# First stage of a streaming encoder step: the scale of tile t+1 ahead of tile t, second halves of the rides two products later, gate columns with hi and lo weights in one stationary

## The reference

```
n = RMSNorm(x) * g_in
z = n @ w_in                      # 2048 x (q, k, v: 3 x 1024; gate: 8; ga, u, gs: 3 x 1024)
logf = log_sigmoid(z[:, gate] + b_f)
# then attention with the cumulated logf, a state-space layer on u, output projections, norms
```

## Time and profile before

| | |
|---|---|
| median of 3 runs | 2473.47 us (2468.51, 2473.47, 2474.2) |
| profiled execution | 2475.24 us, span 2473.5 |
| PE busy | 2272.9 us, 92% of the span |
| LDWEIGHTS busy | 2138.9 us, 86% |
| DVE, ACT, POOL busy | 1593.3, 781.4, 317.3 us |
| mean granted clock of PE | 0.968 |

### The profile page before, as it was taken

How to read it: one execution, slowest core, us unless ns; L and a number is a source line. 1 busy time by engine, 2 the same in 40 slices (tenths; PEclk the granted TensorE clock), 3 DMA queues, 4 the chain that set the end, 5 groups by cost and what they waited for, 6 DMA issues and landing times. The chain is left out here.

```text
span 2473.5 us, 43304 instructions
## 1 busy us (share of the span) xinstructions
PE 2272.9 (92%) x16025; PEld 2138.9 (86%) x16025; DVE 1593.3 (64%) x2934; ACT 781.4 (32%) x1651; POOL 317.3 (13%) x350
## 2 busy tenths in 40 slices
PE   3989999999899999999688877888999999999996
PEld 3989999999899999999577757886888888999996
DVE  6768766776777878884377754755445666334664
ACT  6442333333433333333465534321001113001112
POOL 0011000000112112111233314200001110001110
PEclk9999999999999999999799888998999999999998
DMA  7474444444767788774455524435445446434332
GB/s 236 143 241 113 133 130 129 146 136 136 263 196 213 216 229 229 218 222 128 167 167 172 163 68 181 149 124 175 119 114 164 121 112 200 115 107 130 107 104 97
DMA packets 399412, 390.28 MB, mean 158 GB/s; under 512 B 73896, under 2 KB 341704, under 8 KB 392800
## 3 DMA queue, kind: packets, MB, share of 16 engines
q1 hardware_dynamic: 354176, 271.50, 38.1%
q0 software_dynamic: 20704, 77.95, 9.6%
q10 hardware_dynamic: 24384, 38.87, 4.9%
HBM read 257.56 MB, written 122.01 MB: 153 GB/s over the span
## 5 line engine op out<-in xcount | busy, mean ns | idle before, releaser
L745 PE MATMUL acc<-t_act,w_hi 128*128 128x264 f32 x5376 | 889.3, 288 | 20.0 <-DVE zb L1321 8.0
L745 PEld LDWEIGHTS acc<-t_act,w_hi 128*128 128x128 f32 x5376 | 749.8, 189 | 27.2 <-issue 25.7
L745 PE MATMUL acc<-t_act,w_lo 128*128 128x264 f32 x2688 | 549.0, 286 | 0.0
L2608 PE MATMUL post_acc<-region_hi,w_post_hi 128*128 128x272 f32 (+1 forms) x1536 | 419.0, 327 | 23.7 <-DVE region_lo L2717 19.0
L745 PEld LDWEIGHTS acc<-t_act,w_lo 128*128 128x128 f32 x2688 | 418.0, 189 | 0.0
L2608 PE MATMUL post_acc<-region_hi,w_post_lo 128*128 128x272 f32 (+1 forms) x1536 | 416.1, 325 | 0.0
L2608 PE MATMUL post_acc<-region_lo,w_post_hi 128*128 128x272 f32 (+1 forms) x1536 | 415.4, 325 | 0.0
L1296 DVE TENSOR_TENSOR w_lo<-w_raw_f,w_hi 128x512 fp32r<-128x512 f32 x288 | 198.0, 687 | 164.4 <-ACT w_hi L953 164.2
L2608 PEld LDWEIGHTS post_acc<-region_hi,w_post_hi 128*128 128x128 f32 x1536 | 258.6, 189 | 49.8 <-issue 16.2
L2608 PEld LDWEIGHTS post_acc<-region_lo,w_post_hi 128*128 128x128 f32 x1536 | 259.0, 190 | 22.2
L2608 PEld LDWEIGHTS post_acc<-region_hi,w_post_lo 128*128 128x128 f32 x1536 | 257.5, 190 | 22.8
(11 more groups left out here) (381 smaller groups left out, 3249.1 us busy)
## 6 DMA issues: line engine op xcount, KB each, us to landing
w_raw_f<-in_w_in_dram SPq DMA_DIRECT2D x96, 512.0 KB, 4.0
w_raw<-in_w_out_dram SPq DMA_DIRECT2D x64, 512.0 KB, 4.7
w_raw<-in_w_pg_dram SPq DMA_DIRECT2D x64, 512.0 KB, 4.7
cT<-zb SPq DMA_DIRECT2D x24, 1056.0 KB, 4.3
zb<-cT POOLq DMA_DIRECT2D x96, 264.0 KB, 5.9
zT<-zb POOLq DMA_DIRECT2D x80, 264.0 KB, 3.5
eT<-e_out ACTq DMA_DIRECT2D x16, 528.0 KB, 3.0
t_act<-tS POOLq DMA_DIRECT2D x7, 1056.0 KB, 10.4
```

Of the source, the lines that this page charges most:

```text
L745: mm = pe.matmul(out[:, c, 0:QN], w[:, k, :], t_act[:, SIDE[r], x, k, c * QN:(c + 1) * QN], start=(opens and k == 0 and m == 0), stop=(k = ...
L2608: mm = pe.matmul(acc[b][:, c, 0:width], w[:, k, :], a[region][:, k, start:start + width], start=(k == 0 and n == 0), stop=(k == KD - 1 and ...
```

## The change

There are three parts. In the opening, DVE makes tile t+1's reciprocal and diagonal before it copies and scales tile t, from tile 5 on, and ACT casts the first two sides after tile 5's copy instead of after tile 4's. In the rides, the second half moves from r = 2 to r = 4 on PE, from j = 3 to 5 on ACT and from j = 4 to 6 on DVE; `turn_raw` moves from r = 4 to 2 of pair 2, the exponential on ACT from j = 6 to 2, `powers_one` from j = 6 to 3. For the gate, hi and lo of the 8 columns stand in one stationary, lo 32 columns behind hi, so that two matmuls (x hi and x lo) do what three did (the product of the two lo parts comes with it). The second token half is taken from sides 5 and 4 with the weights w0 + w1 and -w0, which gives x01 w0 + x11 w1 without a snapshot of the first part; the lo rows, at partition 32, are copied by ACT and added by DVE.

```diff
+        WF = 32 + HEADS
+
         def gate_tiles(place, tag):
-            return (place(f"wf_raw{tag}", [P, KD, HEADS]),
-                    *(place(f"{n}{tag}", [P, KD * HEADS + P - HEADS], F32R) for n in ("wf_hi", "wf_lo")),
-                    place(f"f_half{tag}", [HEADS, HN]))
+            return (place(f"wf_raw{tag}", [P, KD, HEADS]), place(f"wf_set{tag}", [P, 4 * KQ, HEADS]),
+                    place(f"wf_two{tag}", [P, 4 * KQ * WF + P - WF], F32R), place(f"f_half{tag}", [HEADS, HN]))
...
                     pe.wait_ge(xb_loaded, 16 * sum(len(list(x_pieces(t))) for i in range(m + 1) for t in (i, i + 5)))
-                if m == 2 and h == 0:
+                if m == 1 and h == 1:
...
-            def gate_part(half, side, h, start):
-                _, hi, lo, _ = wf_tiles[half]
-                for k in range(KQ):
-                    at = ((half * 2 + h) * KQ + k) * HEADS
-                    for m, (w, x) in enumerate(((hi, 0), (hi, 1), (lo, 0))):
-                        for c in range(2):
-                            mm = pe.matmul(oth[:, c, 0:QN], w[:, at:at + P], t_act[:, SIDE[side], x, k, c * QN:(c + 1) * QN],
-                                           start=(start and k == 0 and m == 0), stop=(k == KQ - 1 and m == 2),
-                                           skip_group_check=True)
+            def gate_part(half, sides, first):
+                two = wf_tiles[half][2]
+                for i, side in enumerate(sides):
+                    for k in range(KQ):
+                        at = ((first + i) * KQ + k) * WF
+                        for x in range(2):
+                            for c in range(2):
+                                mm = pe.matmul(oth[:, c, 0:QN], two[:, at:at + P],
+                                               t_act[:, SIDE[side], x, k, c * QN:(c + 1) * QN],
+                                               start=(i == 0 and k == 0 and x == 0), stop=(i == 1 and k == KQ - 1 and x == 1))
...
                         pe.wait_ge(xb_copied, 2 * RIDES)
-                    gate_part(half, 0, 0, True).then_inc(f_part, 1)
+                    gate_part(half, (0, 3), 0).then_inc(f_one, 1)
                 if step == 1:
-                    pe.wait_ge(f_snap, half + 1)
-                    gate_part(half, 3, 1, False).then_inc(f_one, 1)
-                if step == 2:
                     pe.wait_ge(f_one_added, half + 1)
-                    gate_part(half, 1, 0, True)
-                    gate_part(half, 5, 1, False).then_inc(f_two, 1)
+                    gate_part(half, (5, 4), 2).then_inc(f_two, 1)
...
                 pe.wait_ge(small_loaded, 16 * 9)
-                pe.wait_ge(xb_copied, 4)
+                pe.wait_ge(xb_copied, 3)
...
                 for r in range(7):
-                    if 1 <= p <= RIDES and r in (0, 2):
-                        turn_xb(p - 1, r // 2)
-                    if p == 2 and r == 4:
+                    if 1 <= p <= RIDES and r in (0, 4):
+                        turn_xb(p - 1, r // 4)
+                    if p == 2 and r == 2:
                         turn_raw()
-                    if p in GATES and r in (2, 4, 6):
-                        gates(GATES.index(p), r // 2 - 1)
+                    if p in GATES and r in (3, 6):
+                        gates(GATES.index(p), r // 3 - 1)
...
-            def snap_gate(half):
-                act.wait_ge(f_part, half + 1)
-                nc.scalar.copy(quarters(wf_tiles[half][3][:]), oth[0:HEADS, :, 0:QN]).then_inc(f_snap, 1)
+            def snap_gate(half, n):
+                if n:
+                    act.wait_ge(f_two, half + 1)
+                    act.wait_ge(f_one_added, half + 1)
+                else:
+                    act.wait_ge(f_one, half + 1)
+                nc.scalar.copy(quarters(wf_tiles[half][3][:]), oth[32:WF, :, 0:QN]).then_inc(f_snap, 1)
...
                     high_side(4 + j, 4 + j, side_raw[4 + j])
-                if 1 <= p <= RIDES and j in (1, 3):
-                    copy_xb(p - 1, j // 2)
-                if p == 2 and j == 6:
+                if 1 <= p <= RIDES and j in (1, 5):
+                    copy_xb(p - 1, j // 4)
+                if p == 2 and j == 2:
...
                     nc.scalar.activation(q_re[:], tmp[0][:], ACT.Sin).then_inc(cos_done, 1)
-                if p in GATES and j == 3:
-                    snap_gate(GATES.index(p))
+                if p in GATES and j == 4:
+                    snap_gate(GATES.index(p), 0)
+                if p - 1 in GATES and j == 0:
+                    snap_gate(GATES.index(p - 1), 1)
...
                 copy_x(t)
-                if t == 4:
+                if t == 5:
...
             def split_wf(half):
-                raw, hi, lo, _ = wf_tiles[half]
+                raw, full, two, _ = wf_tiles[half]
                 dve.wait_ge(wf_loaded, 16 * (half + 1))
-                nw = KD * HEADS
-                flat = raw.rearrange("p k h -> p (k h)")
-                nc.vector.memset(hi[:, nw:].bitcast(F32), 0.0)
-                nc.vector.memset(lo[:, nw:].bitcast(F32), 0.0)
-                nc.vector.tensor_copy(hi[:, 0:nw], flat).then_inc(wf_hi_done, 1)
+                one, other = (raw[:, (half * 2 + h) * KQ:(half * 2 + h + 1) * KQ] for h in range(2))
+                nw = 4 * KQ
+                cols = two[:, 0:nw * WF].rearrange("p (k m) -> p k m", m=WF)
+                nc.vector.memset(two[:].bitcast(F32), 0.0)
+                nc.vector.tensor_copy(full[:, 0:2 * KQ], raw[:, half * 2 * KQ:(half + 1) * 2 * KQ])
+                TT_(full[:, 2 * KQ:3 * KQ], one, other, ALU.add)
+                link(TS(full[:, 3 * KQ:], one, -1.0, None, ALU.mult))
+                nc.vector.tensor_copy(cols[:, :, 0:HEADS], full[:]).then_inc(wf_hi_done, 1)
                 dve.wait_ge(wf_hi_done, half + 1)
-                TT_(lo[:, 0:nw], flat, hi[:, 0:nw].bitcast(F32), ALU.subtract).then_inc(wf_split, 1)
-
-            def add_gate_one(half):
-                f, out = oth[0:HEADS, :, 0:QN], quarters(lf[:, 0:HN])
-                dve.wait_ge(f_one, half + 1)
+                TT_(cols[:, :, 32:WF], full[:], cols[:, :, 0:HEADS].bitcast(F32), ALU.subtract).then_inc(wf_split, 1)
+
+            def add_gate(half, n):
+                f, out, rest = oth[0:HEADS, :, 0:QN], quarters(lf[:, n * HN:(n + 1) * HN]), quarters(wf_tiles[half][3][:])
+                done = f_added if n else f_one_added
+                dve.wait_ge(f_snap, 2 * half + n + 1)
+                dve.wait_ge(f_two if n else f_one, half + 1)
...
                     dve.wait_ge(past_loaded, 32)
-                    STT(out, f, b_f[:], out, ALU.add, ALU.add).then_inc(f_one_added, 1)
+                    link(STT(out, f, b_f[:], out, ALU.add, ALU.add))
+                    TT_(out, out, rest, ALU.add).then_inc(done, 1)
...
                     dve.wait_ge(xb_used, 2 * RIDES)
-                    nc.vector.tensor_copy(out, f).then_inc(f_one_added, 1)
-
-            def add_gate_two(half):
-                f, out, first = oth[0:HEADS, :, 0:QN], quarters(lf[:, HN:]), quarters(wf_tiles[half][3][:])
-                dve.wait_ge(f_two, half + 1)
-                if half:
-                    link(STT(out, f, b_f[:], out, ALU.add, ALU.add))
-                    TT_(out, out, first, ALU.add).then_inc(f_added, 1)
-                else:
-                    TT_(out, f, first, ALU.add).then_inc(f_added, 1)
+                    TT_(out, f, rest, ALU.add).then_inc(done, 1)
...
                     low_side(4 + j, 4 + j, side_raw[4 + j])
-                if 1 <= p <= RIDES and j in (2, 4):
-                    ride(p - 1, j // 2 - 1)
+                if 1 <= p <= RIDES and j in (2, 6):
+                    ride(p - 1, j // 4)
...
                     add_parts(p - 1)
-                if p == 2 and j == 6:
+                if p == 2 and j == 3:
...
                 if p == 6:
-                    if j == 0:
+                    if j == 1:
...
                         carries()
+                    if j == 4:
+                        add_gate(0, 0)
                     if j == 5:
-                        add_gate_one(0)
...
                 if p == PREP and j == 0:
-                    add_gate_two(0)
+                    add_gate(0, 1)
...
                         split_wf(1)
-                    if j == 5:
-                        add_gate_one(1)
+                    if j == 4:
+                        add_gate(1, 0)
...
                     if j == 0:
-                        add_gate_two(1)
+                        add_gate(1, 1)
...
             dve.wait_ge(g_loaded, 16)
-            for t in range(10):
+            for t in range(5):
...
                 normalize(t)
-                if t >= 5:
-                    sub_tiles(t - 5)
-                if t == 4:
-                    for i, s in enumerate(BUILD[:2]):
-                        low_side(i, s, side_raw[s])
+            spread(5)
+            for i, s in enumerate(BUILD[:2]):
+                low_side(i, s, side_raw[s])
```

(12 more changed lines are left out.)

## The result

Beside the kernel before on one chip the changed kernel took 2455.01 us, median of 5 (2447.23 to 2455.34), against 2468.51, median of 5: ratio 0.9931, 95% interval 0.9912 to 0.9951. Its profiled execution took 2455.19 us, with a span of 2453.5. The forecast, 2461.1, is 6.1 us too high and inside its range; its sum, 12.4 us, stands against 13.5 by these medians.

A forecast was written before the change was run, and what follows sets the result against it. TensorE, busy 92% of the span, was taken as the bound, with gains from idle, needless matmuls and half clock. 3.5 + 8.9 - 1.0 - 4.5 + 7.8 - 2.3 = 12.4 us off 2473.47 gave 2461.1 us; range 2454 to 2469.

The forecast's parts named there:

- the wait for xb_in with its clock: Before pair 4, PE waits 2.9 us for xb_in loads, then loses 1.6 to low clock: 4.5 us given back.
- The stall of pair 3: PE's idle before pair 3's last product, 6.15 us, plus 2.2 at low clock, goes away: 8.35 us gained.
- The level: Starting time from which the forecast difference was taken: the median of the runs before, 2473.47 us.
- The opening: Tiles 5 to 9: waits between diagonal and copy go, less 1.4 us for later casts: 3.5 us net gain.
- Rival (c): The stall returns elsewhere or earlier runs mostly had none: 8.35 us missing, 2469.5 us, no measurable change; chance 0.16.
- remaining wait of 1.1 us on ACT: In pair 3 ACT reaches its copy into xb_t 5.9 us later and waits 1.1 us instead of 7.01.
- Rival (a): The xb_in loads land in time because stores of the ride before moved away: 4.5 us better, 2456.6; chance 0.20.
- raw and powers_one, 1.0 us: Pair 2's second transposes wait until powers_one has read their bank: new PE wait of 1.0 us.
- The gates: 64 fewer matmuls save 7.8 us over two stages; pair 6's wait grows from 2.42 to 4.3, 2.3 given back.
- Rival (b): The split of the gate's weights isn't later for PE than before: 2458.8 us; chance 0.10.
- The clock behind the old gate wait: Pair 6: after PE's 2.42 us wait the 24 gate matmuls take 4.54 us, 1.6 more at low clock.
- Rival (d): Slower: second halves' stores meet the load burst; at 20 us landings four rides lose 34.8 us, 2496; chance 0.04.

The follow-up runs named there:

- before's third: The kernel before run again, nothing edited, for a third trace: no stall in pair 3; one execution, 2464.3 us.
- POOL held: Kernel before; in pair 3 POOL issues its four stores of differences only when ACT's store of the ride's first half has landed: 2470.66 us, single time.
- ACT held for POOL: Kernel before; ACT issues each ride's first-half store only after POOL has issued its two stores of differences: 1.8 +- 2.0 us more than before.

## Why the prediction was right or wrong

**The step that failed** is the wait for xb_in with its clock, put at 4.5 us given back. The runs showed 1.1 us on average and the granted clock at 1.00. The stall of pair 3, put at 8.35 us from one trace, was the other: it is 5.3 us on average, 0 to 9.1 from trace to trace. One was too large a cost, the other too large a gain, and that they nearly cancelled in the sum was luck.

**The level.** "I take the difference off the median, 2473.47" failed: the median of three stood 3.2 us above the mean of 122. That is half of the 6.1 us.

**The opening** was right: 3.65 measured, 3.5 forecast, with the step at 5.60 (5.7 forecast).

**The stall, 8.35 us**, had the right mechanism and the wrong size. In the seven traces whose pair 3 is in the old order, idle time and what the next 24 matmuls take over 2.94 us cost 8.4, 0.6, 0, 9.1, 3.6, 9.0 and 6.8 us: mean 5.3. Rival (c) had this ("the runs of before mostly had none"); by the traces of before itself it is so in two of three. But the forecast's remaining wait of 1.1 us on ACT isn't there, because the store now lands after 6.4 us.

**The xb_in wait, 4.5 us**, was 1.23, 1.39 and 0.69 us, mean 1.1, with no clock lost. I carried over the burst's own times, 2.4 us on SP ahead of the last issue and 9.2 us until it lands. In the changed kernel the last is issued 1.0 us after the first (147.18, 148.16) and lands 9.0 us later: 1.5 us of the wait were time on SP's queue that the new order doesn't have. What shortens it isn't shown; in the two traces of before without a long stall the first two issues took 2.05 and 1.52 us. The clock term copied the case of 2.42 us; the granted clock is 1.00 behind 1.23 us. Rival (a) was nearer, though its words that the same loads cost PE nothing ahead of the pairs before were wrong: PE stood 0.66 us for xb_in at pair 1's turn (91.18) in the trace it was read from.

**raw and powers_one, 1.0 us**: 0.36. DVE's last copy ended at 123.73, which is 127.4 with the opening's 3.65 us added, about as estimated (127.2); PE came at 127.1 instead of 126.3.

By the distance from first product to pair 4's transposes, 98.7 us in seven traces of the old order and 94.6 in eight of the new, the rides' part gives 4.2 us, and 0.6 at pair 5: 4.8, against 8.9 - 1.0 - 4.5 = 3.4. What is left of these errors in the sum is 1.4 us.

**The gates** saved their 7.8 us of matmuls. The wait was forecast at 4.3 and is 4.9, with the memset of 728 columns at 0.67 (forecast 0.7) and add_parts 0.7 us later against PE; the clock costs 2.6, 1.4 and 2.6 us instead of 2.0. From PE's arrival at the gate to the transposes of C it is 29.3 us (four traces) against 33.1 (five), where one product less, 2.94, lies between: 0.8 gained in the first stage, 1.6 forecast. Rival (b) is out. With 3.9 in the second stage: 4.7 instead of 5.5.

The clock behind the old gate wait is itself a draw, which the forecast had as one value. Nine traces have the old gate and a wait of 2.39 to 2.42 us ahead of it. In six the 24 matmuls then took 4.5 us; in three (before's third, POOL held, ACT held for POOL) 3.0 us at a granted clock of 1.00. Before's third trace, PE's timeline and windows:

```profile
215.01 0.75 PE L756 MATMUL oth<-t_act,wf_hia 128*128 128x264 f32 x4 [2.39 <-DVE wf_loa L1483]
...
218.03 0.65 PE L745 MATMUL acc<-t_act,w_hi 128*128 128x264 f32 x4
```

```profile
216.00:220.00 4.00, 4.00 (x36) 4.00 (x35) 3.57 (x9) 0.27 (x1) 1.99 (x3) 1.00 0.78 210
```

Over all nine the stretch is 32.9 us instead of 33.1, and the gain in the first stage 0.6.

**The sum** by what was measured is 3.65 + 4.8 + 4.7 = 13.2 us. 2.1 more in the middle stretch make 15.3, against 16.0 +- 1.0 timed. The forecast had no term for that stretch. Rival (d) didn't occur: no second half's store landed late enough to be seen.

## What to carry to other kernels

A stall read from one trace is one draw: before it is made a term of a sum, look whether it hangs on the moment at which two queues issue, and take a second trace if so; the same holds for the clock lost behind a wait of 2.4 us. A wait that is carried into a new order has to be rebuilt from its parts (issue, queueing, landing), since the old order made some of them. When a stationary is packed fuller, its preparation is what PE meets next: put it a step ahead of the work that it was put behind.

## What the runs showed of the hardware

Of two stores of 256 KB that ACT issued one behind the other, with the same neighbours, the first landed after 4.6 to 6.1 us and the second after 5.9 to 13.0, falling as the moment of issue moved by 1.4 us against POOL's; at a gap shorter still (0.64 us) it was 11.8. Without POOL's stores the second took 7.0 us, without the large store 6.8, without the weights and the large store 5.5.

Behind PE's idle stretches of 0.69 to 1.85 us ahead of pair 4 the granted clock was 1.00 in 160 to 164 us in each of eight traces of the new order, and the turn and its four products took 12.7 us. Behind stretches of 2.30 to 6.93 us ahead of pair 3's last product it fell to 0.50 to 0.72, and 24 matmuls took 4.2 to 5.2 us instead of 2.94. In between one length gave both: behind 2.39 to 2.42 us ahead of the old gate 24 matmuls took 4.5 us in six traces and 3.0 in three.
